# One bank for the heads' norms, three for the products beside the attention core, and the last head's norm beside a four-tile output product

## The reference

```
q = h @ w_q                                   # 8 heads, each of two halves of 64
s = q_half . k_half * 0.125 + bias, causal    # two score maps per head
a = softmax(s0) - lam * softmax(s1)
o = a @ v                                     # 128 per head
o = rms_norm(o, subln_g) * (1 - lambda_init)  # per head, over its 128 channels
y = o.reshape(512, 1024) @ w_o
x = x + g_m * rms_norm(y, norm_g[l, 1])
```

## Time and profile before

| | us |
|---|---|
| median of 3 runs | 2277.66 (2277.59 to 2278.67) |
| profiled execution, its own time | 2286.9 |
| span in the profile | 2285.1 |
| PE busy | 2150.5 (94%) |
| PE weight loads | 1701.3 (74%) |
| DVE busy | 1339.0 (59%) |
| ACT busy | 875.1 (38%) |
| POOL busy | 146.2 (6%) |

### The profile page before, as it was taken

The page is one execution under the profiler, slowest core; times in us unless marked ns, Lnnn a source line. Parts: engine busy times, 40 slices in busy tenths (PEclk is TensorE's granted clock), DMA queues, the critical chain, the costliest instruction groups (busy, mean ns, idle before and its releaser), DMA issues.

```text
span 2285.1 us, 26165 instructions
## 1 busy us (share of the span) xinstructions
PE 2150.5 (94%) x10612; PEld 1701.3 (74%) x10614; DVE 1339.0 (59%) x2273; ACT 875.1 (38%) x1453; POOL 146.2 (6%) x96
## 2 busy tenths in 40 slices
PE   6999889999998999889999998999889999999998
PEld 5755778888887866677888887777555588888886
DVE  5697468847844466547743654468766564633532
ACT  3455434423422255524432433223553433422421
POOL 0463100000010000010000001000000001000000
PEclk9999879999998999979999998999885999999999
DMA  7443225565531220112333222222100032333331
GB/s 270 139 151 97 65 65 192 186 211 166 180 96 49 83 65 29 33 42 79 101 97 97 92 88 66 83 75 65 38 27 1 2 96 80 101 102 92 101 93 65
DMA packets 61752, 214.80 MB, mean 94 GB/s; under 512 B 6848, under 2 KB 7744, under 8 KB 61632
## 3 DMA queue, kind: packets, MB, share of 16 engines
q1 hardware_dynamic: 61632, 213.12, 29.4%
HBM read 211.00 MB, written 2.10 MB: 93 GB/s over the span
## 4 chain that ended last, share of the span: by engine, by line
PE 87%; DVE 7%; ACT 3%; issue 2%; POOL 1%; DMA 0%; SPq 0%; POOLq 0%; DVEq 0%; ACTq 0%
PE bank L285 23%; PE bank L287 23%; PE bank L286 23%; PE bank L290 16%; PE bank L752 2%; DVE wlo L325 1%; DVE steps L805 1%; ACT whi L312 1%; ACT pr L725 1%; DVE tmp L488 0%; DVE Hl L493 0%; DVE sc L1861 0%; POOL small L468 0%; DVE steps L1859 0%; DVE pr L717 0%
## 5 line engine op out<-in xcount | busy, mean ns | idle before, releaser
L285 PE MATMUL bank<-Hh,whi 128*128 128x512 f32 x1632 | 656.5, 402 | 54.9 <-DVE wlo L325 8.4
L287 PE MATMUL bank<-Hh,wlo 128*128 128x512 f32 x1632 | 646.9, 396 | 0.0
L286 PE MATMUL bank<-Hl,whi 128*128 128x512 f32 x1632 | 646.7, 396 | 0.0
L325 DVE TENSOR_TENSOR wlo<-stg,whi 128x1024 fp32r<-128x1024 f32 (+1 forms) x299 | 358.9, 1205 | 438.6 <-ACT whi L312 438.0
L312 ACT ACTIVATE whi<-stg 128x1024 fp32r<-128x1024 f32 (+1 forms) x309 | 314.0, 1026 | 441.5 <-PE bank L287 437.7
L285 PEld LDWEIGHTS bank<-Hh,whi 128*128 128x128 f32 x1632 | 313.6, 192 | 129.2 <-issue 14.2
L287 PEld LDWEIGHTS bank<-Hh,wlo 128*128 128x128 f32 x1632 | 313.2, 192 | 67.7
L286 PEld LDWEIGHTS bank<-Hl,whi 128*128 128x128 f32 x1632 | 314.0, 192 | 62.8 <-issue 0.2
L287 PE MATMUL bank<-HIDh,wlo 128*128 128x512 f32 x352 | 140.4, 399 | 0.0
L286 PE MATMUL bank<-HIDl,whi 128*128 128x512 f32 x352 | 138.7, 394 | 0.0
L285 PE MATMUL bank<-HIDh,whi 128*128 128x512 f32 x352 | 138.0, 392 | 0.0
(11 more groups left out here) (284 smaller groups left out, 2725.6 us busy)
## 6 DMA issues: line engine op xcount, KB each, us to landing
raw<-in_mod_w SPq DMA_DIRECT2D x96, 512.0 KB, 4.2
stg<-in_ffn_in SPq DMA_DIRECT2D x88, 512.0 KB, 4.2
stg<-in_ff SPq DMA_DIRECT2D x64, 512.0 KB, 3.6
stg<-in_ffn_out SPq DMA_DIRECT2D x40, 512.0 KB, 3.6
stg<-in_cm_w SPq DMA_DIRECT2D x24, 512.0 KB, 3.8
stg<-in_gates SPq DMA_DIRECT2D x16, 512.0 KB, 3.5
stg<-in_z_ch SPq DMA_DIRECT2D x12, 512.0 KB, 3.7
stg<-in_w_k SPq DMA_DIRECT2D x8, 512.0 KB, 3.6
```

What stands on the lines that cost most here:

```text
L285: pe.e.matmul(out_, l[0], r[0], start=start, stop=False, skip_group_check=True)
L286: pe.e.matmul(out_, l[0], r[1], start=False, stop=False, skip_group_check=True)
L287: return pe.e.matmul(out_, l[1], r[0], start=False, stop=stop, skip_group_check=True)
L325: hand.e.tensor_tensor(wlo[j % NW][:, 0:n * c], stg[j % NSTG][:, 0:n * c], whi[j % NW][:, 0:n * c].bitcast(F32), ALU.subtract).then_inc(*m ...
```

## The change

- Weight list: the first 512 output columns of the second output product come as two blocks of two heads x 512 columns (heads 4, 5, then 6, 7) in place of two blocks of four heads x 256 columns. The other two blocks stay.
- Banks: the spread of a head's norm goes to NRM, the bank of the sums; so SPREAD is free beside the core, and the products there rotate over 0, 1 and 7.
- After the core PE opens banks 0 to 3 for output tiles 0 to 3, issues head 7's sums, multiplies the four tiles with heads 4 and 5, issues head 7's spread, multiplies with heads 6 and 7. Tiles 4 to 7 follow as two groups in banks 4, 5, 0, 1.
- `high_head` of heads 4, 5, 6 moves into ACT's close of the following head, `low_head` into DVE's close one step later (head 6's right after the core). Head 7's stay after the core.
- DVE's additions of tiles 0 to 3 and ACT's squares of them come together behind the second of the new blocks.

```diff
@@ weight_plan
-    gemm("w_o", 4, DT, range(0, D, 256))
+    plan.extend(("w_o", i, 2, 0, 512) for i in (4, 6))
+    gemm("w_o", 4, DT, [512, 768])
@@ close_pe
-                    spread(f"o{h}", [(dve_done, ("on", h))])
+                    spread(f"o{h}", [(dve_done, ("on", h))], NRM)
@@ tensor
-                rotate_banks([0, 1])
+                rotate_banks([0, 1, SPREAD])
...
-                for i in (4 * H, 4 * H + 2):
-                    close_pe(i)
-                gemm("wo1", "w_o", lambda q: heads_o(4 + q), 4, DT, 4, lambda m: [(dve_done, ("ao", m))])
+
+                rotate_banks([0, 1, 2, 3, 4, 5])
+                into = [acc_bank(("wo1", m), [(dve_done, ("ao", m))]) for m in range(4)]
+                close_pe(4 * H)
+                for i in (4, 6):
+                    j = next_block(pe, "w_o", i)
+                    hi, lo = block_parts(j)
+                    pe.wait_ge(*lo_done(j))
+                    for q in (i, i + 1):
+                        xh, xl, ready = heads_o(q)
+                        pe.wait_ge(*ready)
+                        for m in range(4):
+                            c = slice(m * P, (m + 1) * P)
+                            tok = mm3(into[m][:, :], (hi[:, q - i, c], lo[:, q - i, c]), (xh, xl), q == 4, q == H - 1)
+                            done = [("wo1", m)] if q == H - 1 else []
+                            if q == i + 1 and m == 3:
+                                done.append(("block", j))
+                            if done:
+                                tok.then_inc(*gemm_done.up(*done))
+                    if i == 4:
+                        close_pe(4 * H + 2)
+                gemm("wo1", "w_o", lambda q: heads_o(4 + q), 4, DT, 2, lambda m: [(dve_done, ("ao", m))], 4)
@@ close_dve
-                    dve.e.scalar_tensor_tensor(Qt[:, h, :], Qt[:, h, :], lc[:, 6:7], banks[SPREAD][:, :], ALU.mult,
+                    dve.e.scalar_tensor_tensor(Qt[:, h, :], Qt[:, h, :], lc[:, 6:7], banks[NRM][:, :], ALU.mult,
                                                ALU.mult).then_inc(*dve_done.up(("on", h)))
+                if 4 <= h - 1 < H - 1 and i % 4 == 0:
+                    low_head(h - 1)
@@ vector
-                for i in (4 * H + 1, 4 * H + 2):
-                    close_dve(i)
-                for h in range(4, H):
-                    low_head(h)
+                close_dve(4 * H)
+                close_dve(4 * H + 1)
+                next_block(dve, "w_o", 4)
+                close_dve(4 * H + 2)
+                low_head(H - 1)
+                next_block(dve, "w_o", 6)
...
-                beside_gemm(dve, "w_o", 4, DT, 4, evac)
+                for m in range(4):
+                    evac(m)
+                beside_gemm(dve, "w_o", 4, DT, 2, evac, 4)
@@ close_act
+                    if h > 4:
+                        high_head(h - 1)
@@ scalar
-                for h in range(4, H):
-                    high_head(h)
-                beside_gemm(act, "w_o", 4, DT, 4, lambda m: square("ay", m, Y[m], dve_done["ao", m]))
+                next_block(act, "w_o", 4)
+                high_head(H - 1)
+                next_block(act, "w_o", 6)
+                for m in range(4):
+                    square("ay", m, Y[m], dve_done["ao", m])
+                beside_gemm(act, "w_o", 4, DT, 2, lambda m: square("ay", m, Y[m], dve_done["ao", m]), 4)
@@ sync
-                beside_gemm(sp, "w_o", 4, DT, 4)
+                next_block(sp, "w_o", 4)
+                next_block(sp, "w_o", 6)
+                beside_gemm(sp, "w_o", 4, DT, 2)
```

## The result

The changed kernel takes 2271.85 us (median of 8 runs, 2266.38 to 2275.66) against 2279.07 (2277.59 to 2282.76) for the kernel before: ratio 0.9962, 95% interval 0.9949 to 0.9974, so 8.7 us or 0.4% faster. The forecast was 10.2 us and 2267.5; the saving forecast lies between the two. The first median is 0.35 us above the top of the range, the second inside it.

A forecast was written before the change was run, and what follows sets the result against it. PE was taken to bound the kernel, with 87% of the chain, so time is won where it waits or runs at its lower clock. 3.0 + 4.9 + 2.3 = 10.2 us off the 2277.66 median gave 2267.5, eight-in-ten range 2263.8 to 2271.5.

The forecast's parts named there:

- Part 1 and 2: After the core: head 7's norm hidden, 3.0 us saved; second output product without waits or 1.2 GHz start, 4.9 saved.
- The wait for bank 0: Before head 7's sums: PE waits for ACT's copy of the last tile out of bank 0, 0.88 us lost.
- The spare time of head 7: Second output product: head 7's scaling, copy and low part take 2.4 us under head 6's 2.8 us of matmuls.
- the 1.8 us put down for the lower clock there: Start of the second output product: the 1.2 GHz stretch over 10 matmuls goes, some 1.8 us saved.
- Part 3: Beside the core: three banks instead of two shorten PE's waits at changes of groups, 2.3 us saved.
- The place at 956: Change of groups beside the core: PE's next step waits for DVE, so the third bank saves 0 there.
- Head 6's split ahead of the last copies: At 966, end of the core: the moved head copy delays the copies 0.53 us; net of 0.48, 0.05 lost.
- Part 4: Heads 4, 5, 6 made inside the core and the norms' shared bank: cost 0.
- Rival 1: Beside the core: more banks win nothing, DVE and ACT set the pace; saved 7.9, 2269.8 us; chance 0.2.
- Rival 2: Beside the core: 2.4 GHz kept at group changes, up to 3.2 us more, 2264.3, or one spell more; chance 0.15.
- Its 9.2 us over the median of 2277.66 is taken as unchanged: Base of the sum: profiled execution's 2286.9 us stays 9.2 above the median, from which the saving is subtracted.
- The rule against part 3: Beside the core: a skill's report of no gain from PSUM double-buffering would make part 3 0, the sum 7.9.

The follow-up runs named there:

- from_bank_1: Changed kernel with the second output product's six banks taken in the order 1, 2, 3, 4, 5, 0; 2266.97 us, ratio 0.9941.
- late_spread: Changed kernel with head 7's spread issued behind head 6's products instead of ahead of them; tail 28.7 us against 24.6.
- tail_alone: Kernel before with only the tail's change: two banks beside the core, spread's own bank, heads 4 to 6 split after the core; 2275.03 us, ratio 0.9979.
- late_opening: from_bank_1 with each bank beside the core opened just before its tile's first matmul, first tile's products first; 2267.14 us, ratio 0.9936.
- change_again: The changed kernel itself, unaltered, six more runs in another job with a second trace; 2267.77 us, ratio 0.9947.
- copies_behind: late_opening with head 6 split after the core and, beside the first output product, ACT's next weight split ahead of the two copies; 2262.37 us, ratio 0.9919.

## Why the prediction was right, and where not

- **Part 1 and 2, the tail**: 7.9 us forecast, 8.1 measured (32.7 to 24.6; 8.5 against the second trace before). The wait for bank 0 was put at 0.88, from_bank_1 removes 0.96. The spare time of head 7 was put at 0.3, it is 0.4; late_spread's pause of 2.2 us confirms the chain's length. No wait at the three changes of groups, full grant: both as said. But the 1.8 us put down for the lower clock there hold for the tail and not for the program: over tail_alone's 12 runs the time at 1.2 GHz is on average what it was before.
- **Part 3, three banks**: 2.3 us forecast, 2.7 and 2.9 at equal clock. The mechanism was right. From the first query copy to the matmul behind the pause at 851 it is 29.9 us before and 28.4 after: 1.5 won, where the first change (0.9) and the next (0.48) were put at 1.4. The place at 956 was put at 0, because DVE set the pace there (0.15 us of wait); both traces of the changed kernel have the lower clock behind that pause and no wait for DVE, so TensorE sets the pace and up to 0.5 can be won. That this is the missing 0.5 is read from the traces; no run separates it. Head 6's split ahead of the last copies was sized right (0.53 forecast, pause 0.80 against 0.27).
- **Part 4**: 0 forecast for heads 4 and 5 and for the shared bank; no new wait in the list. What the moved splits are good for was not priced: without them the tail waits 0.3 us more (tail_alone).
- **Rival 1** fell as put (the banks' saving is there), but what it says is true of the next step: with the pause gone altogether, late_opening wins 0.5 of 7.7 us at equal clock.
- **Rival 2**, the clock, is what decides where in the range a run falls. It was given 0.15, its cause was left open, and it was treated as a matter of the core stretch alone. It counted two spells there; the trace has a third and longer one, behind the 3.7 us wait at 916. The first trace of the changed kernel got 6.8 us more of the lower clock there than the first of the kernel before, and that hid all but 0.2 us of part 3's saving. Some luck is in the time too: change_again's six runs hold a mean of some 236 us at 1.2 GHz by their listed clocks, the kernel before's 23 some 247, and at 0.37 to 0.40 us each that is over 4 of the 12.1 us, of which 1.8 were forecast. Whether the change brings this or chance does was not settled: the first eight runs have some 242.
- **A step that did not hold**: "Its 9.2 us over the median of 2277.66 is taken as unchanged". They were not the profile's doing: the second trace of the kernel before comes from an execution of 2276.61 us, with 1272.4 instead of 1280.1 us behind. The three runs shown, 1.1 us apart, were a narrow draw; later runs of the kernel before lie between 2275.97 and 2286.34. The saving of 10.2 us lies between 8.7 and 12.1; the absolute 2267.5 was subtracted from a base that turned out 1.4 to 3 us low.
- **The rule against part 3.** What the Trainium skill reports in "TensorE: Matmul & The Clock Gate", section "HAM oscillation — how this bites in real kernels", "Adding PSUM double-buffering gave no further gain", is a result of one other kernel and not a rule. It does not carry over to this kernel's third bank: 2.7 to 2.9 us at equal clock. Going by the rows was right.

## What to carry to other kernels

A serial chain after the last item of a loop is hidden by the following product as soon as that product can start on the items already finished; that gave three quarters of the saving, and it could be priced to 0.2 us from one trace. Before adding a bank, look at when a bank is opened: opened together, a tile waits that need not, and a rotation that begins with the bank copied last waits for its copy (0.96 us here). And compare stretches of two traces at the same time at 1.2 GHz, from more than one trace of each kernel, before a difference is put down to the change.

## What the runs showed of the hardware

In these 14 traces the lower clock in the core stretch and the tail always began inside a pause of TensorE of over 1 us or at most 1.4 us after its end: at 13 of 13 pauses of 3.7 us, at 29 of 43 of 1.9 to 2.5 us, and not at the same places from one execution to the next. Filling them with unread matmuls kept the grant at 1.00 throughout and shortened the stretch by 5.6 us. The spells also go with the spread of the executions of one kernel, up to 11 us: the slowest of 23 runs of the kernel before (2286.34) has a mean granted clock of 0.943, the fastest (2275.97) 0.947, and the code behind the change, identical in all, took 1272.1 to 1280.1 us, as it held 134.0 to 156.3 us at 1.2 GHz. Whether that share depends on what comes ahead of it was not settled: the four traces with 1278.9 us and more come from the kernel before and from three variants of the change, and the kernel before has 1272.4 in its other trace. Combining filled pauses with copies_behind was not tried.
